# One kernel, three edits: two output buffers in the mixer's last part, a result loaded in three parts, and the first convolution tap on ScalarE

## The reference

```python
h = rms_norm(x, norm_mix_w)
z, xbc, dt_f, dt_b, u_pool, g_a, g_b = split(h @ w_in)
xbc = silu(conv5(xbc) + conv_b)        # centred depthwise convolution over time, 5 taps
y   = scan(xbc, dt_f) + flip(scan(flip(xbc), dt_b)) + d_skip * x
y_a = grouped_rms_norm(y * silu(z)) @ w_ssm_out              # 8 groups of 256 channels
y_b = (mean_pool(u_pool) - u_pool) @ w_pool * pool_scale     # 4 groups, windows 2, 4, 8, 16
x   = x + (sigmoid(g_a) * y_a + sigmoid(g_b) * y_b) @ w_o
x   = x + expert_choice_ffn(rms_norm(x))                     # 16 experts
return rms_norm(x)
```

## Time and profile before

| | |
|---|---|
| time, median of 3 runs | 2678.82 us (2677.99 to 2680.69) |
| the profiled execution | 2680.83 us, span 2679.0 us |
| TensorE busy | 2536.4 us, 95% |
| VectorE busy | 2203.4 us, 82% |
| ScalarE busy | 1506.6 us, 56% |
| DMA | 705.39 MB, mean 263 GB/s |
| mean granted TensorE clock | 0.975 |

### The profile page before, as it was taken

The page is one execution under the profiler, slowest core; times in us unless marked ns, Lnnn a source line. Parts: engine busy times, 40 slices in busy tenths (PEclk is TensorE's granted clock), DMA queues, the critical chain, the costliest instruction groups (busy, mean ns, idle before and its releaser), DMA issues. The chain is left out here.

```text
span 2679.0 us, 33672 instructions
## 1 busy us (share of the span) xinstructions
PE 2536.4 (95%) x13103; PEld 1973.2 (74%) x13103; DVE 2203.4 (82%) x2478; ACT 1506.6 (56%) x1740; POOL 351.1 (13%) x414
## 2 busy tenths in 40 slices
PE   6999999999988989399999999999999999999994
PEld 5888889888977878276767667767767676676673
DVE  5889888898875342689999999999999999999994
ACT  3344444343434121267777777777777777777773
POOL 0322333133410000100000000000000000000001
PEclk9999999999998989599999999999999999999997
DMA  4233223332345333499999999999999999999994
GB/s 152 74 107 126 95 91 105 120 106 88 134 165 185 134 133 124 196 348 379 370 377 377 376 377 367 385 373 380 378 371 374 377 379 373 378 374 369 377 378 160
DMA packets 70797, 705.39 MB, mean 263 GB/s; under 512 B 9344, under 2 KB 13568, under 8 KB 47984
## 3 DMA queue, kind: packets, MB, share of 16 engines
q1 hardware_dynamic: 47216, 628.75, 60.3%
q0 software_dynamic: 14064, 55.94, 6.7%
q10 hardware_dynamic: 9360, 18.55, 1.8%
HBM read 669.16 MB, written 34.06 MB: 262 GB/s over the span
## 5 line engine op out<-in xcount | busy, mean ns | idle before, releaser
L1984 DVE TENSOR_TENSOR wl<-raw,wh 128x2048 fp32r<-128x2048 f32 x528 | 1194.1, 2290 | 117.7 <-ACT wh L1923 107.2
L1923 ACT ACTIVATE wh<-raw 128x2048 fp32r<-128x2048 f32 x528 | 990.8, 1911 | 258.6 <-PE p_y L2073 224.9
L2046 PE MATMUL p_gu<-wh,xh 128*96 128x512 f32 x1408 | 566.9, 403 | 3.0 <-DVE xl L1990 3.0
L2046 PE MATMUL p_gu<-wh,xl 128*96 128x512 f32 x1408 | 556.0, 395 | 0.0
L2046 PE MATMUL p_gu<-wl,xh 128*96 128x512 f32 x1408 | 553.9, 393 | 0.0
L861 PE MATMUL pp<-h_hi,wx_hi 128*128 128x256 f32 (+1 forms) x864 | 307.7, 356 | 1.4 <-ACT fo L520 1.4
L2046 PEld LDWEIGHTS p_gu<-wl,xh 128*96 128x96 f32 x1408 | 227.6, 162 | 100.4
L2046 PEld LDWEIGHTS p_gu<-wh,xh 128*96 128x96 f32 x1408 | 227.8, 162 | 91.8 <-DVE wl L1984 4.6
L861 PE MATMUL pp<-h_hi,wx_lo 128*128 128x256 f32 (+1 forms) x864 | 293.7, 340 | 0.0
L861 PE MATMUL pp<-h_lo,wx_hi 128*128 128x256 f32 (+1 forms) x864 | 292.9, 339 | 0.0
L2046 PEld LDWEIGHTS p_gu<-wh,xl 128*96 128x96 f32 x1408 | 227.8, 162 | 83.5
(11 more groups left out here) (247 smaller groups left out, 3704.2 us busy)
## 6 DMA issues: line engine op xcount, KB each, us to landing
raw<-in_w_e SPq DMA_DIRECT2D x176, 3072.0 KB, 11.0
w_raw<-in_w_x SPq DMA_DIRECT2D x48, 512.0 KB, 3.5
dec<-acs POOLq DMA_DIRECT2D x48, 512.0 KB, 4.9
w_raw<-in_w_g SPq DMA_DIRECT2D x24, 512.0 KB, 3.5
gx<-fo ACTq DMA_DIRECT2D x24, 384.0 KB, 2.6
g_tab<-gx POOLq DMA_DIRECT2D x8, 1152.0 KB, 5.9
w_raw<-in_w_s SPq DMA_DIRECT2D x16, 512.0 KB, 3.4
ys<-yt ACTq DMA_DIRECT2D x14, 384.0 KB, 2.8
```

Of the source, the lines that this page charges most:

```text
L1923: act.activation(wh[:, n % 2, at:at + hi - lo], raw[:, n % RAW, lo:hi], ACT.Copy).then_inc(s_wh, 1)
L1984: dve.tensor_tensor(wl[:, n % 2, to], raw[:, n % RAW, lo:hi], wh[:, n % 2, to].bitcast(F32), ALU.subtract).then_inc(s_wl, 1)
L2046: mm = pe.matmul(p_gu[n % 2][0:SLOTS, 0:w], xx[:, side, k * SLOTS:(k + 1) * SLOTS], ww[:, n % 2, k * w:(k + 1) * w], start=(k == 0 and i = ...
```

## The change

- Results 16 and later alternate between `fo` and `yt`, the staging tile of the turned y, each with a semaphore of its own (`out_buf`, `out_slot`, `stored_before`, `out_free`, `m_fo[0]` and `m_fo[1]`). The first use of `yt` waits for the stores of y.
- The order `LAST` becomes `..., p3, 20, 21, p2, 22, p1, 23, p0`: each pair of maps but the first comes one fill later, and the last fill stands ahead of p0. The orders of ScalarE and VectorE follow. The PSUM slot of a late fill follows its place in the order.
- `load_y` is cut in three: groups 0 and 1 when the scan is over, 2 and 3 after `pooled_low(1)`, 4, 5 and 6 after `pooled_low(2)`; `y_lo[6]` gets another room, and `y_high(6)` takes over the wait for the last map.
- The six `turn_y` of group 7 go into two half banks by turns (`pyt7`) and all stand in the first tile of the final product, at inner steps 0, 2, 4, 6, 8 and 10; before, three stood in fill 23 and three at steps 2, 5 and 8.
- The first tap of each convolution is an Identity activation on ScalarE with a scale and a bias per partition (`first_tap`), right behind the copy into `pad` (for j = 0 in a group turn after `rows(gs, 5)`). VectorE's `conv(g, 0)` now stands whole behind `weighted(gs, 3)`, `decayed(gs, 0)` and `masked_cb(gs, 5)`. `tanh_conv(g, 0)` moves behind `high(weight(g, 5))`.

```diff
-LAST = (14, 15, 16, 17, 18, 19, "p3", 20, "p2", 21, "p1", 22, "p0", 23)
+LAST = (14, 15, 16, 17, 18, 19, "p3", 20, 21, "p2", 22, "p1", 23, "p0")
+SHARED = EARLY + 2
+        out_buf = (fo[:], yt[:].rearrange("p i n -> p (i n)"))
+        pyt7 = (pst[:, 0, :], poff[:, 0, :])
+        def out_slot(n):
+            return (n - SHARED) % 2 if n >= SHARED else 0
+        def stored_before(n):
+            return 16 * (n if n < SHARED else (n - SHARED) // 2 + (0 if out_slot(n) else SHARED))
...
-            for g in range(G - 2):
-                load_y(g)
-            pool.wait_ge(s_proj, mapped_in(0, 1))
-            load_y(G - 2)
+            load_y(0)
+            load_y(1)
+            pool.wait_ge(s_pl, 2)
+            load_y(2)
+            load_y(3)
+            pool.wait_ge(s_pl, 3)
+            load_y(4)
+            load_y(5)
+            load_y(6)
             pool.wait_ge(s_pl, 4)
...
+            def out_free(n):
+                if stored_before(n):
+                    act.wait_ge(m_fo[out_slot(n)], stored_before(n))
+                if n == SHARED + 1:
+                    act.wait_ge(s_ysp, 32 * (G - 1))
+            def first_tap(g, j):
+                w0 = j * (TAPS + 1)
+                if j == 0 and not is0(g):
+                    act.wait_ge(s_tr, 6 * g)
+                    act.wait_ge(s_ct, g)
+                act.wait_ge(s_pad, 4 * g + (j + 1))
+                act.activation(u[:, j, :], pad[:, j % 2, 0:CONV_OUT], ACT.Identity,
+                               scale=conv_tab[:, g, w0:w0 + 1], bias=conv_tab[:, g, w0 + TAPS:w0 + TAPS + 1])\
+                   .then_inc(s_tap0, 1)
...
                 rows(gs, 5)
+                first_tap(g, 0)
                 turned_y(gy, 5)
                 high(weight(g, 3))
-                tanh_conv(g, 0)
                 to_pad(g, 1)
+                first_tap(g, 1)
                 high(weight(g, 4))
                 high(weight(g, 5))
+                tanh_conv(g, 0)
                 decay(gs, 2)
                 to_pad(g, 2)
+                first_tap(g, 2)
                 high(fill_weight(f))
...
                 pool_out(3, 1)
-                high(pool_weight(2))
+                high(fill_weight(21))
                 pool_store(3, 1)
                 square(gs, 5)
+                fill_out(20)
+                high(pool_weight(2))
+                fill_store(20)
                 pooled_high(1)
-                fill_out(20)
-                high(fill_weight(21))
-                fill_store(20)
+                fill_out(21)
+                high(fill_weight(22))
+                fill_store(21)
                 pool_out(2, 0)
...
                 pooled_high(2)
                 y_high(0)
+                y_high(1)
+                fill_out(22)
+                high(fill_weight(23))
+                fill_store(22)
+                y_high(2)
                 pool_out(1, 0)
                 pool_store(1, 0)
+                y_high(3)
                 pool_out(1, 1)
                 high(pool_weight(0))
                 pool_store(1, 1)
                 pooled_high(3)
+                y_high(4)
+                fill_out(23)
+                high(ssm_weight(0))
+                fill_store(23)
+                y_high(5)
                 pool_out(0, 0)
...
                 weighted(gs, 2)
-                conv(g, 0, 0, 1)
                 masked_cb(gs, 4)
-                conv(g, 0, 1, 3)
                 weighted(gs, 3)
+                decayed(gs, 0)
                 masked_cb(gs, 5)
-                conv(g, 0, 3)
-                decayed(gs, 0)
+                conv(g, 0)
                 low(weight(g, 3))
```

More of the change, by code:

```diff
@@ L518, in pool_out @@
                 act.wait_ge(s_proj, mapped_in(q, i))
-                act.wait_ge(m_fo, 16 * n)
-                act.activation(fo[:], pp[n % 2][:, 0:T], ACT.Copy, scale=pscale[:, 2 * q + i:2 * q + i + 1]).then_inc(s_fe, 1)
+                out_free(n)
+                act.activation(out_buf[out_slot(n)], pp[n % 2][:, 0:T], ACT.Copy,
+                               scale=pscale[:, 2 * q + i:2 * q + i + 1]).then_inc(s_fe, 1)
             def pool_store(q, i):
-                act.wait_ge(s_fe, EARLY + last_outputs(f"p{q}") + i + 1)
-                act.dma_start(gx[2 * q + i, 2], fo[:]).then_inc(m_fo, 16)
+                store(gx[2 * q + i, 2], EARLY + last_outputs(f"p{q}") + i)
             def pooled_high(n):
@@ L751, in last @@
                 pooled_high(3)
-                y_high(1)
-                y_high(2)
-                fill_out(22)
-                high(fill_weight(23))
-                fill_store(22)
-                y_high(3)
+                y_high(4)
[3 more added lines that the diff above has]
+                y_high(5)
                 pool_out(0, 0)
@@ L760, in last @@
                 pool_out(0, 1)
-                high(ssm_weight(0))
+                high(ssm_weight(1))
                 pool_store(0, 1)
                 y_high_turned(0)
-                y_high(4)
                 y_high_turned(1)
-                y_high(5)
+                y_high(6)
                 y_high_turned(2)
-                fill_out(23)
-                fill_store(23)
-                high(ssm_weight(1))
                 y_high_turned(3)
-                y_high(6)
                 y_high_turned(4)
@@ L816, in _ @@
             to_pad(0, 2)
+            first_tap(0, 2)
             tanh_conv(0, 2)
@@ L875, in fill @@
                     pe.wait_ge(s_wl, fill_weight(k) + 1)
-                rows(k, fill_weight(k), part)
+                rows(k if k < EARLY else EARLY + last_outputs(k), fill_weight(k), part)
             def pool_map(n, i):
@@ L1042, in last @@
                 fill(20, 2)
-                pool_map(1, 0)
-                pool_map(1, 1)
-                for k in (21, "p1", 22, "p0", 23):
-                    if k == "p1":
-                        pool_map(2, 0)
-                        pool_map(2, 1)
-                    elif k == "p0":
-                        pool_map(3, 0)
-                        pool_map(3, 1)
-                    else:
+                for k in (21, "p2", 22, "p1", 23, "p0"):
+                    if isinstance(k, int):
                         for part in range(3):
                             fill(k, part)
-                            if k == 23:
-                                turn_y(gs, part)
+                    else:
+                        pool_map(POOL_ORDER.index(int(k[1])), 0)
+                        pool_map(POOL_ORDER.index(int(k[1])), 1)
                 for i in range(KD):
@@ L1067, in scan_out @@
                         kk = half * KD + k
-                        if i == 0 and kk in (2, 5, 8):
-                            turn_y(gs, 2 + (kk + 1) // 3)
+                        if i == 0 and kk in (0, 2, 4, 6, 8, 10):
+                            turn_y(gs, kk // 2)
                         if i == 0:
@@ L1356, in both @@
                 silu(g, 0)
-                conv(g, 1, 0, 2)
+                conv(g, 1, 1, 3)
                 combine(gs, 0, ycs)
-                conv(g, 1, 2)
+                conv(g, 1, 3)
                 decayed(gs, 2)
@@ L1364, in both @@
                 spans(gs, 3)
-                conv(g, 2, 0, 3)
+                conv(g, 2, 1, 3)
                 combine(gs, 2, ycs)
@@ L1373, in both @@
                 combine(gs, 3, ycs)
-                conv(g, 3, 0, 3)
+                conv(g, 3, 1, 3)
                 spans(gs, 5)
```

101 lines of the change are left out of this document (54 added, 47 removed).

## The result

The changed kernel takes **2652.22 us** (median of 4 runs, 2651.87 to 2653.12), the kernel before 2678.99 (4 runs, 2677.99 to 2680.69): ratio 0.9899, 95% interval 0.9884 to 0.9914, 26.8 us less. The forecast was 2645, so 33.5 us less; the range 2640 to 2660 holds the result, the forecast's own range of 2640 to 2650 does not. The profiled execution took 2652.45 us, with a span of 2650.3.

The account below looks back on a forecast made before the run. TensorE's sequence was taken as the path, its idle and the slow clock behind it as the possible gain. Terms of -23.5 and -10 us sum to -33.5, from 2678.8 to 2645; own range 2640 to 2650, all cases 2640 to 2660.

Parts of the forecast that it names:

- Term 1: Last part, fill 20 to final product: TensorE's idle and slow clock go, final product starts 24.0 us earlier; -23.5 us net.
- the shortest such distance is about 3.5 us, against 2.5 to land: Last part, two buffers: a copy waits for the store two outputs earlier, which should land in time.
- the 0.7 that I had allowed: Last part: two small new waits, `y_high(2)` ahead of `pool_out(1, 0)` and `y_high(5)` ahead of `pool_out(0, 0)`; together 0.7 us.
- the idle ahead of the maps of group 2: Last part, at 793.76: 5.65 us of TensorE idle, laid to the single output buffer's copy waiting for a store.
- Term 2: Group turns: first tap on ScalarE closes TensorE's wait ahead of `output(gs, 0)`, 1.47 us in 7 turns; -10 us, bounds 0 and 10.5.
- 1.55 us earlier: Group turn: VectorE loses a 0.6 us tap and a 0.95 us wait, so the copy `carry(gs, 3)` ends at 313.55.
- 0.1 to spare: Group turn: margin in us by which VectorE's copy would be ready before TensorE could start `output(gs, 0)`.
- Rival 1: Group turns: the wait stays because VectorE's operations lengthen beside POOL or the fill weight comes late; 2655; chance 0.13.
- Prologue: Before the turns: ScalarE's first two taps lie under the 10.8 us step-size product, costing nothing; uncovered, 2 us.
- Rival 2: Last part closes only partly: a late `ys` load delays `y_high`, holding `fill_out(22)` and `fill_out(23)`; 8 us back, 2653; chance 0.12.
- Rival 3: Group turns: slower through ScalarE table switches at each first tap, six a turn; 2650 to 2704; chance 0.03.
- The list of signs: What the profile after should show, in turns, last part, stores, `ys` loads and table loads, if the forecast held.

Follow-up runs that it names:

- Experiment 7: The changed kernel with the third and fourth load of `ys` held until the store of fill 21's result has landed; 2650.30 us, ratio 0.9894.
- Experiment 3: The changed kernel with one output buffer for all late results, new order and the rest kept; 2663.88 us, ratio 0.9939.
- experiment 1: The kernel before with only the first tap on ScalarE and the new places of `conv(g, 0)` and `tanh_conv(g, 0)`; 2670.63 us, ratio 0.9966.
- experiment 9: Both mends: the changed kernel with those `ys` loads held for the store and the copy `carry(gs, 3)` ahead of the fill weight's low half; 2643.43 us.
- after: The changed kernel itself, against the kernel before; 2652.22 us, ratio 0.9899.
- experiment 4: The changed kernel with all seven loads of `ys` issued at once; 2652.39 us, ratio 0.9899.
- experiment 6: The kernel before with `conv(g, 0)`, all taps on VectorE, moved behind `weighted(3)`, `decayed(0)` and `masked_cb(5)`; 2677.92 us, ratio 0.9995.
- experiment 10: The kernel of experiment 9 with all convolution taps on VectorE as before; 2651.51 us without one slow execution, 2652.74 with it; run again, 2649.98.

## Why the prediction was right, and where it was off

The forecast was right in sign, in place and in both mechanisms, and 7 us too good: 33.5 us against 26.8. Of the 28.7 us between the two profiled executions 2.5 lie where the forecast had nothing, 1.2 in the prologue and 1.3 behind the mixer; that these made the miss smaller is luck.

**Term 1, the last part: -23.5, measured 18.5** (18.8 less 0.3 by the timelines; 17.1 as the part alone). The step that failed is "the shortest such distance is about 3.5 us, against 2.5 to land". The distance was right, 3.3 us from the issue of the store to the end of the maps whose result needs its buffer (791.87). The landing was not. I took the median of the stores, though the same row gave 7.2 as the worst and though I had written that this wait falls where `ys` is in flight: the two stores issued beside those loads in the kernel before, at 792.56 and 800.51, took 6.9 and 7.2. The store took 7.5. The 5 us that are missing are: 2.66 and 0.59 us of idle, 0.16 for each of these two by which matmuls no longer overlap, 1.6 for fill 23, 10.1 instead of 8.4 us at a granted clock of 0.83 behind the idle, 0.1 for the maps of group 1 and 0.3 between the last map and the first turned tile; together 5.6, less the 0.7 that I had allowed. Experiment 7 shows it: with that store freed, the two idles close and the stretch is 4.4 us shorter. The stretch took 43.6 us where I gave 38.5. The three `turn_y` moved into the final product cost 0.3 us, 0.5 predicted, and none waits.

One attribution was wrong, without harm to the sum. I had put the idle ahead of the maps of group 2, too, to the single buffer. Experiment 3 has one buffer and no such idle; it was `pooled_low(1)` behind the old order. The sum held because my placing of the new order had that low half in time for its own reasons; to lay all of the idle to one cause was wrong.

**Term 2, the group turn: -10, measured 7.8** (8.3 as the part alone). The step that failed is "1.55 us earlier": VectorE's list did lose them, but "0.1 to spare" held only if nothing else got longer. Two groups of operations took 0.84 us longer in their new place beside GpSimd, the later taps 0.41 shorter, and of the 1.47 that I closed 1.11 closed: 7 x 0.36 = 2.5 us, the difference of 10.3 and 7.8. The trace of before could have told that lengths depend on the place: it has `weighted` at 2.20 and, in the same turn at 303.88, at 1.13 us. Rival 1 named that mechanism and gave it the whole term; it took a quarter. The first tap itself takes 1.04 us at the median of 32, beside 1.0 predicted from L544 and L600.

**Prologue: 0, measured 1.2 gained** in the profiled execution, and lost in others. Where the turns began 2 us late, in experiments 1 and 9, it was not the taps that were uncovered: `acT` came within 0.4 us of when it had come before, and TensorE was ahead of it. That wait stands in two of eight profiled executions with the tap on ScalarE and in none of the five readable ones without; whether the tap has a part in it is not shown.

**Rival 2** (the `ys` traffic, 8 us back) was the nearest: the place was right, the way was not. No `ys` load was late, their median was 7.8 us; a store was, and it landed in time once two of the loads were held back (experiment 7). The estimate of 8 us back stands against 5. **Rival 3** (table switches) did not come. The execution of after still has one load:

```profile
L845 ACT ACT_TABLE_LOAD x1 | 1.3, 1283 | 3.8 <-issue 3.8
```

The Trainium skill, "ScalarE: Activation LUTs", section "Table sets", has identity in every set, and the trace agrees: one load, at 32 ScalarE instructions more.

**The list of signs.** "No idle ahead of the first product of `output(gs, 0)`": 2.1 us in seven turns are left. "A stretch near 38.5 us at clock 1.00": 43.6 at 0.96. "No copy of ScalarE waiting for a store": wrong, 5.42 and later 2.78 us; the second cost TensorE nothing. "y loads landing in well under 12 us": 7.8 at the median, but by experiment 4 that is worth nothing. "One table load": right.

## What to carry to other kernels

A second buffer frees the engine only if the store of the first lands in time. Take for its landing what stores take beside the transfers that will be in flight then, not the median of the whole execution; and where bulk loads and a small store that somebody waits for meet, hold the loads back by a wait rather than reorder the engines behind the store (4.4 us of the stretch against 1.0 here; the medians of these two alone don't tell them apart). Before an operation goes to another engine, ask whether the one that the bottleneck waits for could simply stand one place earlier in its list: here one moved line was worth as much as the tap's move. And an earlier place in a list is not free when another engine's work lies beside it: price the operations there by rows from there.

## What the runs showed of the hardware that I had not expected

- Some operations of VectorE are longer where GpSimd's multiplies run: four 128x128 `scalar_tensor_tensor` took 1.13 us where GpSimd was idle and 2.20 to 2.99 where it was not, one 128x512 `tensor_tensor` 0.68 and 1.10. It goes the other way too: VectorE's low half of the weights (128x1024) took 1.23 us beside GpSimd and 1.22 alone, and GpSimd's two `xw` multiplies that ran beside it took 2.21 us, against 1.28. The numbers 2.62 and 1.10 came alike in after and in experiment 6, and 2.63 and 1.10 in experiment 1.
- A store of 384 KB landed after 7.5 us with four loads of `ys` ahead of it, after 7.6 with seven, and after 3.4 with two. How the loads and the store share the DMA engines doesn't follow from these three.
- TensorE's granted clock in one stretch of the prologue (69 to 77 us), behind idle, was 0.59 in the execution before, 0.65 in after and 1.00 in the one with both mends. Where it was 1.00, a wait of 3.1 us stands behind it and then a clock of 0.50 to 0.70 up to 92 us, so the gain doesn't reach the end.
- In one execution of the kernel of experiment 10 the whole took 8978.79 us, with VectorE's and ScalarE's operations as long as ever and TensorE's longer. The groups of its expert stage, with TensorE's mean of 1120 ns against 402 in the page of after, and ScalarE's unchanged, and then the clock on record:

```profile
L2086 PE MATMUL p_gu<-wh,xh 128*96 128x512 f32 x1164 | 1304.1, 1120 | 2.1 <-DVE xl L2030 2.1
...
L1963 ACT ACTIVATE wh<-raw 128x2048 fp32r<-128x2048 f32 x438 | 819.8, 1906 | 1397.9 <-PE p_y L2113 1363.7 <-PEq L2141 34.2
```

```profile
core 0: 8977.0 us, clock 1.000
```

  The granted clock reads 1.000 in it, so it does not tell of this. The same kernel ran again at 2649.98; I have no cause for it.
